# Moving the memory's norm out of the last projections of layer 1 and into its first branch, in a two-block transformer kernel on one core

## The chip, the core and the metric

The kernel runs on one core of a Trainium2 chip. The core has a TensorE for matrix products (PE in the profile, its weight loads PEld), a VectorE (DVE), a ScalarE (ACT), a GpSimd (POOL) and a SyncE (SP), whose queue issues the transfers. The engines run beside each other and wait for each other by semaphores. The metric is the device time of one execution in microseconds, lower is better. The kernel before takes 2549.95 us, the median of three runs that lie between 2549.95 and 2549.96.

## What is computed

The reference is two blocks, one behind the other, over 256 tokens of width 1024, all in float32.

```
x = first_block(x, c, ctx, c_ctx, ...)          # 2 hybrid layers, x and ctx of 256 tokens each
return second_block(x, mem_2, ...)              # 2 layers with a cross attention to a memory
```

A layer of the first block norms its tokens, projects them, and runs three branches: A (a gated recurrent attention with 4 heads), B (a differential attention with 8 heads) and C (a Fourier mix). A branch ends in a merge, a gate times an output projection, and the three merges are summed and go through one last projection `w_out` whose result, gated, is added to x:

```
x = x + gate * merge(y_a, y_b, y_c, mg, w_a_out, w_b_out, w_c_out, w_out)
```

The second block reads a memory of 256 tokens in every layer:

```
def rms_norm(x, g):
    y = xf * lax.rsqrt(jnp.mean(xf * xf, axis=-1, keepdims=True) + EPS)
    return y * g
for i in range(DEPTH):
    h = rms_norm(x, g_mix[i]);  x = x + mixer(h)
    x = x + memory_cross_attention(rms_norm(x, g_xq[i]), rms_norm(mem, g_mem[i]), w_xq[i], w_xkv[i], w_xo[i])
    x = x + swiglu(rms_norm(x, g_ffn[i]), w_gate_up[i], w_down[i])
```

The memory does not depend on x, so its norm can be made at any time once it has arrived. Only the scale `g_mem` differs between the two layers.

## The kernel before

All activations are held transposed: a tensor is eight chunks k of 128 features by the tokens. Every product is made in three passes, with each operand split into a high part (rounded, `wh`, `HYh`) and a low part (the rest, `wl`, `HYl`): high by high, high by low, low by high. A chunk of a projection is so 8 x 3 = 24 matmuls of 256 columns.

The weights are packed into units of up to 1 MB, in the order of use. SP loads a unit into one of two `raw` slots (L2765) when the low part of the unit two before is done. ScalarE rounds it to `wh` (L1332, L1333) when the TensorE has used the unit two before, and VectorE makes `wl` (L1883, L1885). In the programs of both engines this is `used(tag, j)`: the unit has been used, so convert the one two behind it. A unit of a projection is 48 matmuls.

Each engine has its own program, written out in order: `tensor_program`, `scalar_program`, `vector_program`, `pool_program`, `sync_program`. What stands in the order is what runs; nothing is rearranged. An engine waits with `wait_ge` for a named event of another one and with `wait_own` for its own last instruction. The helpers `tt`, `ts`, `stt` (VectorE) and `act` (ScalarE) record nearly every instruction on one line each (L1864, L1868, L1872 and L1322), so the trace is read by tiles. `X` holds x; in layer 1 of the first block its left half is free and holds the memory (`MT`), loaded at the beginning of the layer.

Layer 1 of the first block, as far as it matters here:

- Branch A, heads h = 0 to 3. Per head the TensorE does `a_pick` and `a_s` (scores), two chunks of a gate `a_o` into banks 0 and 1, two chunks `a_z` into the same banks, the products `a_out`, and the next head's `a_qk` and `a_v`. A bank is free for `a_z` when ScalarE has taken its `a_o` with a tanh. Before that tanh ScalarE makes the exponentials of the scores, which wait for VectorE's mask additions (`TM<-PS,colC,T`).
- Its merge, steps j = 0 to 7, one unit each.
- Branch B with its merge, branch C with its merge.
- `project_out`: eight chunks of `w_out`, two to a unit j = 0 to 3. VectorE updates `X` with each chunk (`X<-PS,ada,X`); ScalarE makes from it the high part and the square for the next norm `gmix0`, VectorE the low part and the sum of squares. Chunk k + 2 waits for the update of chunk k.

The memory's norm (`gmem`) also stands in `project_out`: after unit 1 ScalarE squares the memory in four pieces of 512 columns, `memory_root` adds them in three steps and makes the inverse root from the TensorE's `sums`; after chunk 5 the TensorE spreads the root over a bank, and `memory_normed` multiplies the eight chunks (`X<-X,PS`). `memory_high(0)` on ScalarE (eight `HYh<-X,V`) stands ahead of the updates' own high parts of unit 3, and `memory_low(0)` on VectorE (eight `HYl<-X,V,HYh`) at the end of `project_out`. The TensorE then begins the second block with the first key projection of the memory, `memory(0, 0, ...)`, a unit of 48 matmuls that reads these parts chunk by chunk, and the sums of `gmix0` behind it.

## Time and profile before

| | |
|---|---|
| median of 3 runs | 2549.95 us |
| profiled execution, its own time | 2551.46 us |
| its span, first to last instruction | 2549.6 us |
| TensorE busy | 2369.0 us, 93% |
| VectorE busy | 1334.0 us, 52% |
| ScalarE busy | 1027.2 us, 40% |
| GpSimd busy | 252.2 us, 10% |
| mean granted clock of the TensorE | 0.962 |
| share of the TensorE in the chain that ended last | 77% |

A row of the timeline gives the start, the duration, the engine, the line, the operation with what it writes and reads, the count of merged instructions, and in brackets the engine's idle time before it with what ended that. The busy time of the TensorE includes time at a low clock: granted clock 1.00 is 2.4 GHz and 0.50 is 1.2 GHz, and a mean in between is a mix of the two.

### The profile page before, as it was taken

To read this page: it belongs to the slowest core of one execution; us is meant where nothing else is said; L and a number is where in the kernel's file an instruction comes from. 1 tells how busy PE (TensorE), PEld (TensorE's weight loads), DVE (VectorE), ACT (ScalarE), POOL (GpSimd) and SP (SyncE) were. 2 spreads that over 40 slices of the span, in tenths; PEclk is the share of its full clock that TensorE was granted. 3 is DMA by queue.
4 is the path that set the end of the run, shared out by engine and by line. 5 is a ranking of instruction groups with operands and counts; after the bars stand their busy time and mean duration, and the time that the engine had idled before them with its cause. 6 is when DMAs were issued, how large, how long until landed. Compare 5 with 4: busy or idle time off the path is not lost.

```text
span 2549.6 us, 38388 instructions
## 1 busy us (share of the span) xinstructions
PE 2369.0 (93%) x16176; PEld 2128.6 (83%) x16176; DVE 1334.0 (52%) x2731; ACT 1027.2 (40%) x1962; POOL 252.2 (10%) x260
## 2 busy tenths in 40 slices
PE   5999999999979999899999999978888999888998
PEld 3888779888758988699998889978678999767998
DVE  5544424677433223555456654466555555565554
ACT  2433322444422222444434454443444443453543
POOL 1000002222001111000023301201000100100110
PEclk7999999999999999899999999989999999898999
DMA  6321143111224222232332234453132544312544
GB/s 245 101 68 67 57 174 135 67 67 67 83 81 157 75 70 98 74 117 99 129 137 83 70 114 149 166 163 121 51 126 105 182 167 165 114 50 87 179 172 142
DMA packets 50412, 291.45 MB, mean 114 GB/s; under 512 B 8960, under 2 KB 13312, under 8 KB 19072
## 3 DMA queue, kind: packets, MB, share of 16 engines
q1 hardware_dynamic: 50240, 289.00, 31.6%
q8 instruction: 127, 2.08, 0.3%
q14 instruction: 45, 0.37, 0.0%
HBM read 286.89 MB, written 2.36 MB: 113 GB/s over the span
## 4 chain that ended last, share of the span: by engine, by line
PE 77%; DVE 14%; ACT 5%; DMA 2%; issue 1%; POOL 0%; SPq 0%; DVEq 0%; ACTq 0%; POOLq 0%
PE PS L492 75%; DVE wl L1883 2%; PE PS L496 2%; DVE wl L1885 2%; DMA raw<-in_wpk 2%; ACT wh L1332 2%; DVE TM L1864 1%; ACT TM L1322 1%; ACT TMG L1322 1%; DVE colS L1872 1%; DVE HYl L1872 1%; DVE TMG L1872 1%; DVE TM L1872 1%; ACT HYh L1322 1%; DVE colS L2343 1%
## 5 line engine op out<-in xcount | busy, mean ns | idle before, releaser
L492 PE MATMUL PS<-HYh,wh 128*128 128x256 f32 (+1 forms) x3000 | 959.5, 320 | 53.0 <-DVE HYl L1872 35.8
L492 PE MATMUL PS<-HYl,wh 128*128 128x256 f32 (+1 forms) x3000 | 944.3, 315 | 0.0
L492 PE MATMUL PS<-HYh,wl 128*128 128x256 f32 (+1 forms) x3000 | 943.2, 314 | 0.0
L1883 DVE TENSOR_TENSOR wl<-raw,wh 128x1280 fp32r<-128x1280 f32 (+2 forms) x254 | 369.2, 1453 | 596.2 <-ACT wh L1332 596.1
L492 PEld LDWEIGHTS PS<-HYh,wh 128*128 128x128 f32 x3000 | 585.3, 195 | 96.8 <-DVE HYl L1872 38.3
L492 PEld LDWEIGHTS PS<-HYh,wl 128*128 128x128 f32 x3000 | 584.7, 195 | 31.1
L492 PEld LDWEIGHTS PS<-HYl,wh 128*128 128x128 f32 x3000 | 585.6, 195 | 29.5
L1332 ACT ACTIVATE wh<-raw 128x1280 fp32r<-128x1280 f32 (+2 forms) x254 | 306.7, 1208 | 378.3 <-PE PS L492 251.2
L492 PE MATMUL PS<-wh,HYh 128*128 128x256 f32 x1458 | 424.6, 291 | 17.2 <-DVE HYl L1872 11.2
L492 PE MATMUL PS<-wh,HYl 128*128 128x256 f32 x1458 | 415.4, 285 | 0.0
L492 PE MATMUL PS<-wl,HYh 128*128 128x256 f32 x1458 | 415.4, 285 | 0.0
L1322 ACT ACTIVATE TM<-PS 128x512 f32<-128x512 f32 (+4 forms) x339 | 163.7, 498 | 556.7 <-PE PS L492 426.7
L492 PEld LDWEIGHTS PS<-wh,HYh 128*128 128x128 f32 x1458 | 282.2, 194 | 23.0 <-DVE HYl L1872 12.0
L492 PEld LDWEIGHTS PS<-wl,HYh 128*128 128x128 f32 x1458 | 282.4, 194 | 0.3
L492 PEld LDWEIGHTS PS<-wh,HYl 128*128 128x128 f32 x1458 | 282.0, 193 | 0.1
L1885 DVE TENSOR_TENSOR wl<-raw,wh 128x768 fp32r<-128x768 f32 (+2 forms) x254 | 248.1, 977 | 0.0
L492 PE MATMUL PS<-TM 128*128 128x128 f32 (+6 forms) x992 | 218.4, 399 | 19.8 <-ACT rows L1322 8.5
L1333 ACT ACTIVATE wh<-raw 128x768 fp32r<-128x768 f32 (+2 forms) x254 | 206.8, 814 | 0.0
L492 PEld LDWEIGHTS PS<-TM 128*128 128x128 f32 (+2 forms) x992 | 145.5, 194 | 53.9 <-issue 11.9
L2617 POOL TENSOR_TENSOR HYl<-TM,HYh 128x256 fp32r<-128x256 f32 (+2 forms) x56 | 54.9, 982 | 610.9 <-ACT HYh L1322 610.9
L1322 ACT ACTIVATE TMG<-PS 128x512 f32<-128x512 f32 (+2 forms) x121 | 53.4, 441 | 133.2 <-PE PS L492 119.5
L1322 ACT ACTIVATE TMG<-PS,colS 128x512 f32<-128x512 f32 (+1 forms) x104 | 62.1, 603 | 83.2 <-DVE colS L1868 82.9
(181 smaller groups left out, 1793.2 us busy)
## 6 DMA issues: line engine op xcount, KB each, us to landing
raw<-in_wpk SPq DMA_DIRECT2D x235, 1024.0 KB, 4.8
raw<-in_wpk SPq DMA_DIRECT2D x32, 704.0 KB, 4.0
TM<-in_wpk SPq DMA_DIRECT2D x4, 1024.0 KB, 17.4
X<-in_xin SPq DMA_DIRECT2D x1, 2048.0 KB, 9.3
Y<-in_wpk SPq DMA_DIRECT2D x2, 1024.0 KB, 23.1
Y<-bias_d SPq DMA_DIRECT2D x4, 512.0 KB, 9.8
raw<-in_wpk SPq DMA_DIRECT2D x3, 512.0 KB, 3.7
T<-in_tabs SPq DMA_DIRECT2D x1, 1216.0 KB, 15.0
```

Source lines behind the costliest of these rows:

```text
L492: return P.x.matmul(o, l, r, start=start, stop=stop)
L496: return P.x.transpose(o, i, ident[0:p, 0:p])
L1322: return A.x.activation(o, i, f, **kw).then_inc(*act_step.mark(*events))
L1332: A.x.activation(wh[:, s, 0:c], raw[:, r, 0:c], ACT.Copy).then_inc(*hi_split.mark((u, 0)))
L1333: A.x.activation(wh[:, s, c:n], raw[:, r, c:n], ACT.Copy).then_inc(*hi_split.mark((u, 1)))
L1864: return D.x.tensor_tensor(o, a, b, op).then_inc(*dve_step.mark(*events))
L1872: return D.x.scalar_tensor_tensor(out=o, in0=a, scalar=s, in1=b, op0=op0, op1=op1).then_inc(*dve_step.mark(*events))
L1883: D.x.tensor_tensor(wl[:, s, 0:c], raw[:, r, 0:c], wh[:, s, 0:c], ALU.subtract).then_inc(*lo_split.mark())
L1885: D.x.tensor_tensor(wl[:, s, c:n], raw[:, r, c:n], wh[:, s, c:n], ALU.subtract).then_inc(*lo_split.mark(u))
L2343: D.x.reduce_max(mx, src, AX).then_inc(*dve_step.mark())
L2617: return G.x.tensor_tensor(o, a, b, op).then_inc(*pool_step.mark(*events))
```

## The change

The squares of the memory are made in layer 1's branch A, one piece per head, and added up there. They no longer have a place of their own in `TM` (columns 512 to 2560) but use the right halves of `a_g` and `a_z`, which are free in layer 1. Sums, root, spread and normalisation stand in the merge of branch A. In `project_out` the eight high parts come at once, ahead of the first conversion, and one low part with every chunk.

```diff
-        n_sq, n_x = TM[:, 512:2560].rearrange("p (k t) -> p k t", k=8), tm(2560, [8, 256])
+        n_x = tm(2560, [8, 256])
+        g_sum, g_sq = a_g[:, :, 256:512], a_z[:, :, 256:512]
@@ tensor_program, merge
+                    if l == 1 and br == "a" and j == 2:
+                        P.wait_ge(dve_step, ("gmem", "squares", 3))
+                        sums(6, [g_sum[:, 0], g_sum[:, 1]], 256, o1024[:, 0:1], 1, 0, ("gmem", "sums"))
+                    if l == 1 and br == "a" and j == 4:
+                        P.wait_ge(dve_step, ("gmem", "root"))
+                        spread(6, colS[:, 60:62], 256, 1, 0, ("gmem", "spread"))
@@ tensor_program, branch_b
-                free[6] = (dve_step, ("ada", 14)) if l == 0 else (dve_step, ("a_h", l, 3, 3))
+                free[6] = (dve_step, ("ada", 14)) if l == 0 else (dve_step, ("mem", 7))
@@ tensor_program, project_out
-                        if l == 1 and 2 * j + h == 3:
-                            P.wait_ge(dve_step, ("gmem", "squares"))
-                            sums(6, [n_sq[:, 0], n_sq[:, 1]], 256, o1024[:, 0:1], 1, 0, ("gmem", "sums"))
-                        if l == 1 and 2 * j + h == 5:
-                            P.wait_ge(dve_step, ("gmem", "root"))
-                            spread(6, colS[:, 60:62], 256, 1, 0, ("gmem", "spread"))
@@ scalar_program, branch_a, at the end of head h
+                    if l:
+                        A.wait_ge(mem_in, "all")
+                        if h >= 2:
+                            A.wait_ge(dve_step, ("gmem", "squares", h - 1))
+                        act(g_sq if h else g_sum, MT[:, 2 * h:2 * h + 2], ACT.Square, ("gmem", "square", h))
@@ scalar_program, project_out
+                    memory_high(0)
                     for j in range(4):
                         A.wait_ge(projected, ("w_out", l, 2 * j + 1))
                         used("w_out", 4 * l + j)
-                        if j == 1:
-                            for i in range(4):
-                                A.wait_ge(mem_in, "all")
-                                act(n_sq[:, 2 * i:2 * i + 2], MT[:, 2 * i:2 * i + 2], ACT.Square, ("gmem", "square", i))
-                        if j == 3:
-                            memory_high(0)
@@ scalar_program, memory_high
-                    if l:
-                        A.wait_ge(projected, ("w_out", 1, 7))
+                    A.wait_ge(projected, ("w_out", 1, 7) if l else ("m_value", 1, "c", 7))
@@ vector_program, branch_a, at the end of head h
+                        if l and h:
+                            memory_squares(h)
+            def memory_squares(h):
+                D.wait_ge(act_step, ("gmem", "square", 0))
+                D.wait_ge(act_step, ("gmem", "square", h))
+                D.wait_own(dve_step)
+                tt(g_sum, g_sum, g_sq, ALU.add, ("gmem", "squares", h))
@@ vector_program, merge
+                    if l == 1 and br == "a":
+                        if j == 0:
+                            memory_squares(3)
+                        if j == 3:
+                            memory_root()
+                        if j == 5:
+                            memory_normed()
@@ vector_program, project_out
                         if h and (l or j < 3):
                             used("w_out", 4 * l + j)
-                        if l == 1 and k == 3:
-                            memory_root()
-                        if l == 1 and k == 5:
-                            memory_normed()
                         if l == 1:
+                            memory_low(0, k)
...
                 if l == 1:
                     low("gmix0", 7)
-                    memory_low(0)
```

The order of VectorE's instructions around chunks 4 and 5 of `project_out`. `X<-PS,ada,X` is the update of a chunk, the two `wl` rows a conversion, `HYl<-X,V,HYh` a low part, `TM<-TM` an addition of squares. Before:

```order
L1872 SCALAR_TENSOR_TENSOR X<-PS,ada,X 128x256
L1872 SCALAR_TENSOR_TENSOR HYl<-X,V,HYh 128x256
L1864 TENSOR_TENSOR TM<-TM 128x256
L1872 SCALAR_TENSOR_TENSOR X<-PS,ada,X 128x256
L1883 TENSOR_TENSOR wl<-raw,wh 128x1280
L1885 TENSOR_TENSOR wl<-raw,wh 128x768
L1864 TENSOR_TENSOR X<-X,PS 128x256 x8
L1872 SCALAR_TENSOR_TENSOR HYl<-X,V,HYh 128x256
```

And now:

```order
L1872 SCALAR_TENSOR_TENSOR X<-PS,ada,X 128x256
L1872 SCALAR_TENSOR_TENSOR HYl<-X,V,HYh 128x256 x2
L1864 TENSOR_TENSOR TM<-TM 128x256
L1872 SCALAR_TENSOR_TENSOR X<-PS,ada,X 128x256
L1883 TENSOR_TENSOR wl<-raw,wh 128x1280
L1885 TENSOR_TENSOR wl<-raw,wh 128x768
L1872 SCALAR_TENSOR_TENSOR HYl<-X,V,HYh 128x256 x2
L1864 TENSOR_TENSOR TM<-TM 128x256
```

The normalisation of eight is gone, and every chunk has two low parts, the first of the memory and the second of the update before.

The end of `project_out` on VectorE, from the update of chunk 7 on. Before:

```order
L1872 SCALAR_TENSOR_TENSOR X<-PS,ada,X 128x256
L1883 TENSOR_TENSOR wl<-raw,wh 128x1280
L1885 TENSOR_TENSOR wl<-raw,wh 128x768
L1872 SCALAR_TENSOR_TENSOR HYl<-X,V,HYh 128x256
L1864 TENSOR_TENSOR TM<-TM 128x256
L1872 SCALAR_TENSOR_TENSOR HYl<-X,V,HYh 128x256 x9
```

And now:

```order
L1872 SCALAR_TENSOR_TENSOR X<-PS,ada,X 128x256
L1883 TENSOR_TENSOR wl<-raw,wh 128x1280
L1885 TENSOR_TENSOR wl<-raw,wh 128x768
L1872 SCALAR_TENSOR_TENSOR HYl<-X,V,HYh 128x256 x2
L1864 TENSOR_TENSOR TM<-TM 128x256
L1872 SCALAR_TENSOR_TENSOR HYl<-X,V,HYh 128x256
```

Of the memory's eight low parts only that of chunk 7 is left behind the conversion, as the first of the two in its row.

In branch A the additions of squares come between a head's last conversion and the next head's mask additions (`TM<-PS,colC,T`). VectorE, between two heads, now:

```order
L1864 TENSOR_TENSOR HYl<-TM,HYh 128x2x256
L1883 TENSOR_TENSOR wl<-raw,wh 128x1280
L1885 TENSOR_TENSOR wl<-raw,wh 128x768
L1864 TENSOR_TENSOR TM<-TM 128x2x256
L1872 SCALAR_TENSOR_TENSOR TM<-PS,colC,T 128x128 x4
```

The fourth row is new; before, the mask additions followed the conversion.

## Rows read from the trace of the kernel before

**Rows 1.** By stretch: length, busy PE PEld DVE ACT POOL, PEclk, DMA share, GB/s

```profile
1641.00:1656.00 15.00, 15.00 (x127) 15.00 (x127) 8.87 (x15) 7.40 (x13) 2.32 (x3) 1.00 0.50 178
1656.80:1660.80 4.00, 1.47 (x13) 1.27 (x12) 3.27 (x5) 0.93 (x3) 1.58 (x1) 1.00 0.10 41
1669.20:1691.60 22.40, 16.05 (x108) 15.85 (x108) 14.44 (x34) 8.91 (x16) 0.00 (x0) 0.77 0.29 102
1691.60:1706.60 15.00, 7.22 (x48) 7.25 (x49) 9.56 (x20) 6.61 (x14) 0.00 (x0) 0.77 0.99 256
1245.00:1249.00 4.00, 3.91 (x20) 3.91 (x21) 1.60 (x3) 0.94 (x3) 0.00 (x0) 0.57 0.00 0
```

**Rows 2.** Timeline of the TensorE: start, duration, what, count, idle before, releaser

```profile
1675.52 1.87 PE L492 MATMUL PS<-T,TM 128*128 128x1 f32 x8 [6.33 <-DVE TM L1864]
...
1699.38 0.55 PE L492 MATMUL PS<-HYh,wh 128*128 128x256 f32 x1 [7.81 <-DVE HYl L1872]
...
1699.95 0.42 PE L492 MATMUL PS<-HYh,wl 128*128 128x256 f32 x1
1700.16 0.41 PE L492 MATMUL PS<-HYh,wh 128*128 128x256 f32 x1
...
1706.61 0.95 PE L492 MATMUL PS<-T,TM 128*128 128x1 f32 x8
...
1245.09 1.07 PE L496 MATMUL PS<-T,TM 128*128 128x128 f32 x4 [2.85 <-ACT TM L1322]
```

**Rows 3.** Timeline of VectorE in the last projections of layer 1

```profile
1664.78 1.49 DVE L1883 TENSOR_TENSOR wl<-raw,wh 128x1280 fp32r<-128x1280 f32 x1 [0.82 <-ACT wh L1332]
1666.19 0.95 DVE L1885 TENSOR_TENSOR wl<-raw,wh 128x768 fp32r<-128x768 f32 x1
1667.06 0.48 DVE L1872 SCALAR_TENSOR_TENSOR HYl<-X,V,HYh 128x256 fp32r<-128x256 f32 x1
1667.45 0.48 DVE L1872 SCALAR_TENSOR_TENSOR X<-PS,ada,X 128x256 f32<-128x256 f32 x1
1668.04 0.48 DVE L1872 SCALAR_TENSOR_TENSOR HYl<-X,V,HYh 128x256 fp32r<-128x256 f32 x1
1668.62 0.42 DVE L1864 TENSOR_TENSOR TM<-TM 128x256 f32<-128x256 f32 x1
...
1673.19 2.27 DVE L1864 TENSOR_TENSOR TM<-TM 128x512 f32<-128x512 f32 x3
...
1689.00 2.73 DVE L1864 TENSOR_TENSOR X<-X,PS 128x256 f32<-128x256 f32 x8
...
1698.35 3.65 DVE L1872 SCALAR_TENSOR_TENSOR HYl<-X,V,HYh 128x256 fp32r<-128x256 f32 x9
```

**Rows 4.** Timeline of ScalarE in the last projections of layer 1

```profile
1658.41 0.42 ACT L1322 ACTIVATE HYh<-Y 128x256 fp32r<-128x256 f32 x1 [1.10 <-POOL Y L2617]
1663.47 1.27 ACT L1332 ACTIVATE wh<-raw 128x1280 fp32r<-128x1280 f32 x1 [4.64 <-PE PS L492]
...
1669.61 1.27 ACT L1332 ACTIVATE wh<-raw 128x1280 fp32r<-128x1280 f32 x1 [2.72 <-DMA raw<-in_wpk]
...
1671.52 2.17 ACT L1322 ACTIVATE TM<-X 128x512 f32<-128x512 f32 x4
```

**Rows 5.** Timelines of VectorE and ScalarE in branch A and its merge

```profile
1182.05 0.95 DVE L1885 TENSOR_TENSOR wl<-raw,wh 128x768 fp32r<-128x768 f32 x1
1182.91 1.12 DVE L1872 SCALAR_TENSOR_TENSOR TM<-PS,colC,T 128x128 f32<-128x128 f32 x4
...
1269.04 1.49 DVE L1883 TENSOR_TENSOR wl<-raw,wh 128x1280 fp32r<-128x1280 f32 x1 [3.07 <-ACT wh L1332]
...
1186.35 0.42 ACT L1322 ACTIVATE TM<-PS 128x256 f32<-128x256 f32 x1
1187.15 0.39 ACT L1322 ACTIVATE TM<-PS 128x256 f32<-128x256 f32 x1 [0.38 <-PE PS L492]
```

**Rows 6.** Issue to landing of the unit issued at 1697.0, by the raw tile

```profile
DMA to landing us min/median/max: 9.2/9.2/9.2
```

More of the change, by code:

```diff
@@ L2294, in memory_root @@
             def memory_root():
-                D.wait_ge(act_step, ("gmem", "square", 0))
-                for i in range(1, 4):
-                    D.wait_ge(act_step, ("gmem", "square", i))
-                    D.wait_own(dve_step)
-                    tt(n_sq[:, 0:2], n_sq[:, 0:2], n_sq[:, 2 * i:2 * i + 2], ALU.add, ("gmem", "squares"))
                 D.wait_ge(pe_step, ("gmem", "sums"))
@@ L2306, in memory_normed, with memory_low @@
                     tt(MT[:, k], MT[:, k], bank(6)[:, 0:256], ALU.mult, ("mem", k))
-            def memory_low(l):
-                for k in range(8):
+            def memory_low(l, *ks):
+                for k in ks:
                     D.wait_ge(act_step, ("mem_hi", l, k))
@@ L2447, in self_attention @@
                     if i == 0:
-                        memory_low(1)
+                        memory_low(1, *range(8))
                 D.wait_ge(pe_step, ("ab_q_spread", 1))
```

## The prediction

> **What bounds the kernel now.** I read three views in this order: the busy time by stretch, the timeline of the TensorE around the last projections of layer 1, and then the timelines of the two engines that feed it. The kernel is bound by the TensorE: away from waits it issues a matmul of 256 columns every 0.12 us (127 in 15 us, clock 1.00) [rows 1], and every other engine has idle time. So a change is worth what it takes out of the TensorE's own idle time and low clock. The stretch from 1669.2 to 1706.6 us holds the two places that the diff touches. The reader is to see two things in [rows 1, 2]. The first: after chunk 3 of the output projection the TensorE stands still for 6.33 us, then does the sums of the memory's squares, and ends chunk 7 at 1691.6. The second: it stands still again for 7.81 us until the first low part of the memory is there, and ends the first key projection (48 matmuls) at 1706.6. Both stretches have a mean clock of 0.77, between the two levels of 1.2 and 2.4 GHz [rows 1]. The work in between is 4 chunks and one unit of 48, that is 6 x 24 matmuls x 0.12 = 17.3 us; 37.4 us pass. At most 20.1 us can be had here.
>
> Why it waits is in [rows 3, 4]. The squares are made on ScalarE at 1671.5, after a conversion that had waited until 1669.6 for its transfer; VectorE adds them in three steps (2.27 us). The second wait is for ScalarE's eight high parts and VectorE's eight low parts (one row of 9, 3.65 us), both queued behind a conversion.
>
> **The change part by part.**
>
> *Taken out of the projections.* No squares, sums, root or normalisation is left between chunk 3 and chunk 6. Chunk 4 can start at 1669.2, if its weights and its bank are there: the weights were converted from 1664.8 to 1667.1 [rows 3], and VectorE's update of chunk 2 (1667.45 in the row) was out by 1668. So 6.33 us of idle, the sums at a cold clock, and the slow matmuls behind them go.
>
> *High parts at once.* Eight ScalarE instructions stand ahead of the first conversion now. ScalarE's last merged high part starts at 1658.4, and the conversion waits until 1663.5 for the TensorE (4.64 us of idle) [rows 4]. Eight at about 0.41 take 3.3 us, so they end at 1662.1. Cost nothing; the cover has 1.4 us left.
>
> *Low parts by chunk.* This is what is late next, so I put VectorE's queue together from start to start. From [rows 3]: update to low part 0.59, low part to addition 0.58, low part to update 0.39, first half of a conversion to the second 1.41, second half to the next 0.87. A low part of the memory without a wait takes 0.40 (3.65 / 9), and the next instruction, which waits for its own engine, comes 0.58 behind it. An update or an addition starts its successor 0.09 before its own end where that doesn't wait (0.48 against 0.39), so addition to update is 0.33 to 0.35. An even chunk is 0.40 + 0.58 + 0.58 + 0.35 = 1.91 us, an odd one with its conversion 0.39 + 1.41 + 0.87 + 0.58 + 0.58 + 0.35 = 4.18, together 6.1, against 5.76 of the TensorE for two chunks. VectorE falls behind a little. Run through from 1660.6 with ScalarE's conversions as they stand, the updates start at 1668.0 (chunk 2), 1669.9, 1674.7, 1676.6, 1680.8, 1682.7 (chunk 7). Chunk 6 needs the update of chunk 4, out at 1675.2 where the TensorE arrives at 1675.0: it ends chunk 7 at 1681.0. The key projection needs the update of chunk 6: it starts at 1681.35. Its matmuls take the memory in order of k; the last low part stands behind the conversion that follows chunk 7 (1683.1 and 1684.5, then 1685.4) and is out at 1685.9, where the TensorE wants it at 1683.9: a wait of 2.0 us. Then 27 matmuls: the unit ends at 1689.15. Before it ended at 1706.6. **Gain 17.5 us.** The bound from one side is 20.1 (no new wait), from the other 10.9 - 0.5 = 10.4 (the second wait stays whole: 22.4 us less 4 x 2.88, less the small waits).
>
> *Squares in the first branch.* Four ScalarE instructions of 128x512 at about 0.6 (2.17 / 4) [rows 4]; each stands where ScalarE then waits over 1.4 us, so they cost nothing. Three additions of VectorE at 0.7 to 0.8 (2.27 / 3). The third falls in the merge. The first two stand between the second half of a conversion and the mask additions of the next head (1182.1 and 1182.9 [rows 5]), and what follows moves by 0.8: ScalarE's exponentials, then its tanh of gate chunk 0 at 1186.35, which frees bank 0 only at 1187.6 where it was 1186.8. The TensorE wants that bank when the other chunk ends, at about 1187.0 (its tanh starts at 1187.15). So it waits some 0.7 us where it waited for nothing, in two heads: **1.4 us lost.** The bounds are 0, if the bank is asked for later than I read, and 2 x 0.83 = 1.7. Behind ScalarE wait only the next tanh and a conversion. A conversion takes 3.7 us from the end of a unit to the weights (1663.5 to 1667.1 [rows 3, 4]) and its unit is wanted 5.76 after it: 2 us of slack.
>
> *Sums, root, normalisation in the merge.* The sums are 8 passes in 0.95 us at the full clock (those of the next norm at 1706.6 [rows 2]); with the half as many passes of the spread, 0.45, that is **1.3 us lost** there, with 0.9 and 2.3 (the same sums took 1.87 at the low clock) as bounds. They are already counted as gone from the projections. VectorE idles 3.07 us in every unit of the merge [rows 5]; the root (12 small ones, 0.2 each, 2.35 us) and the normalisation (8 in 2.73 us [rows 3]) each stand alone in such a gap. The cover is 0.3 us at the tighter one, and a conversion late by less than 2 us still meets its unit. Nothing. The wait for bank 6 in front of the second branch is moved to the last normalised chunk, which is out two units earlier.
>
> *Transfers.* Everything on SP's queue that hangs on a conversion comes with it. The one that can be late is the unit that stands behind the four bias blocks: before it took 9.2 us [rows 6]. Now it goes out at 1685.5, when its conversion is done, and closer behind those blocks: I add 2 us, an estimate, and it is in by 1696.7, where ScalarE wants it at about 1696.1 (1689.15, the norm's sums 0.95, a unit 5.76, a copy). The slack of 2 us takes that up. Nothing.
>
> **Sum.** 17.5 - 1.4 - 1.3 = 14.8 us. The profiled execution has a span of 2549.6 and took 2551.46, 1.5 above the median of the runs; the difference is taken off the median: 2549.95 - 14.8 = **2535.1 us**.
>
> The clock, as a test of the 2.0 us wait: after 2.5 us of idle at 1657 the stretch 1656.8 to 1660.8 (1.47 us busy) still has 1.00 [rows 1]; after the 2.85 us at 1245 [rows 2] the next 4 us have 0.57. My waits are shorter than the first, so I keep the full clock; two gaps of that size (1245, 1657) now come at another time and may fall either way, about 2 us each.
>
> **Rivals.**
> *The clock falls in the new wait.* The key projection lost 7.23 - 5.76 = 1.5 us to it before [rows 2]; 27 matmuls all at half speed would be 2.5. 2537. For it speaks that three short waits fall within 8 us.
> *The second wait stays.* VectorE's low parts and ScalarE's copies collide more than I have them, and the TensorE still waits as long at the key projection: gain 10.4, less 2.7: 2542.2. Against it: seven of eight low parts now have a slot ahead of chunk 7's end.
> *No new waits.* The last low part is in time and the heads hide the additions: 2.0 + 0.5 + 1.4 more: 2531.2.
> *The transfer hides it.* Chunk 4 waits for weights instead, and the moved work is pure cost: 2549.95 + 2.7 = 2552.6. Against it: 1667.1 in the row.
> *Slower, by the clock.* VectorE needs 6.1 us for two chunks where the TensorE needs 5.76, so from chunk 4 on the TensorE has a short wait in every chunk. If that pattern held the clock at its low level until the fourth projection of the second block is done (12 chunks, 288 matmuls at 0.213, the distance of the two rows at 1700 [rows 2], for 0.12), it would cost 26.8 us: 2561.9. It decides from the point where it lasts beyond 6 chunks or so. Against it stand the short waits of 0.3 us beside a wait of 2.5 us at clock 1.00 in the row.
> The Trainium skill (TensorE: Matmul & The Clock Gate, A second HAM failure mode: psum-queue depth-cycling) describes a kernel in which frequent short idles between groups of matmuls made the clock go to and fro; by that rule this rival would be the likely one. The trace here shows the full clock across a longer wait than any that I expect, so I give it little.
>
> **How the numbers follow.** My forecast 0.68 (its own range 2532.5 to 2537.5), the clock in the new wait 0.12, the second wait 0.08, no new waits 0.06, the transfer 0.03, slower by the clock 0.03. The range to hold 8 in 10 takes in the two coins of the clock and leaves out the last two and a part of the second wait: 2530.5 to 2541. Within 0.2% (5.1 us, about what can be told from no change) lies only the transfer case: 0.03; slower 0.03; faster 0.94.
>
> **What would show it.** After: no TensorE wait between chunk 3 and chunk 5 of layer 1's projections; all eight chunks end within 23.5 us of the start of the first; one wait of about 2 us inside the first key projection, ended by a low part on VectorE; 17 to 18 us less up to its end; two waits of 0.7 us in the last two heads of the branch, ended by ScalarE's tanh; 1.3 us of sums and spread in the merge. I am wrong if the TensorE still waits over 4 us at the key projection, if the stretch from 1669 on shows a clock under 0.9, or if the branch and its merge grow by over 4 us.

## The result, and where the time went

The changed kernel took 2535.56 us (median of 4 runs, 2533.26 to 2538.65) beside a median of 2549.95 for the kernel before (a fourth run of that one took 2555.34). The ratio is 0.994, with a 95% interval of 0.9924 to 0.9955. Five more runs of it, made later beside the experiments, gave a median of 2535.24 (2534.43 to 2539.52), and the ratio there is 0.9934 (0.9921 to 0.9946): the kernel before had a median of 2552.6 in that round, 17.4 more. The forecast was 2535.1.

The profiled execution of the changed kernel is the slowest of the first four: it took 2538.65, its span is 2536.8 against 2549.6, 12.8 less. Before the spans are read, one has to know how much of a difference belongs to the edit. I laid the TensorE instructions of the two traces against each other, one by one, and read how much later or earlier the same instruction starts after the change (positive is later):

| stretch, in the times of before | changed kernel | the same kernel, profiled again |
|---|---|---|
| start to 1095 us (nothing changed in it) | +1.6 | +0.2 |
| 1095 to 1285, branch A's last heads and the merge's start | +2.4 | +0.9 |
| 1285 to 1640 | 0.0 | -1.1 |
| 1640 to 1727, the projections and the first key projection | -17.8 | -17.4 |
| 1727 to the end | +0.9 | +0.4 |
| sum, from unrounded terms | -12.8 | -17.0 |

The second column is the run "again" of the next section. Only the fourth line is the edit's gain and the second its price. In the first column the price is read at a like clock (both kernels had 3.4 us of low clock in the second stretch); in the second column that low clock is absent, which takes 1.5 us off the price. I put the rest down to the clock, granted otherwise from run to run. For the third line that is argued only: of the twelve profiles in which the norm is early, nine have 13.7 us of low clock there and start 0.9 to 1.3 us less late behind it, and three have 17.1 us like the kernel before and the one other profile with the norm in its old place. Whether the edit has a part in that, no run here tells.

By stretch the profile after shows this (columns as in [rows 1]):

```profile
1640.00:1673.20 33.20, 30.67 (x256) 30.47 (x255) 20.23 (x31) 18.02 (x33) 5.03 (x5) 1.00 0.56 199
1673.20:1692.90 19.70, 17.83 (x146) 17.31 (x145) 16.63 (x29) 10.26 (x18) 0.00 (x0) 1.00 0.72 220
```

The second line, with the PEclk third from its end, runs from the end of chunk 3 to the end of the key projection, and it answers to the third and fourth of [rows 1]: 19.7 us where 37.4 passed. The granted clock is 1.00, the higher of the two levels, where it was 0.77. The TensorE's timeline there (start, duration, what, count, idle before, releaser), answering to [rows 2]:

```profile
1663.61 0.39 PE L493 MATMUL PS<-HYh,wh 128*128 128x256 f32 x1 [2.53 <-DVE HYl L1864]
...
1689.55 0.38 PE L493 MATMUL PS<-HYh,wh 128*128 128x256 f32 x1 [1.79 <-DVE HYl L1872]
...
1692.87 0.95 PE L493 MATMUL PS<-T,TM 128*128 128x1 f32 x8
```

These are the start of chunk 0, the one wait left behind it, and the next norm's sums. The waits of 6.33 and 7.81 us are gone. What released the wait of 1.79 us stands in VectorE's timeline, which answers to [rows 3]:

```profile
1684.84 1.06 DVE L1872 SCALAR_TENSOR_TENSOR HYl<-X,V,HYh 128x256 fp32r<-128x256 f32 x2
1686.01 0.42 DVE L1864 TENSOR_TENSOR TM<-TM 128x256 f32<-128x256 f32 x1
1686.35 0.47 DVE L1872 SCALAR_TENSOR_TENSOR X<-PS,ada,X 128x256 f32<-128x256 f32 x1
1686.75 1.48 DVE L1883 TENSOR_TENSOR wl<-raw,wh 128x1280 fp32r<-128x1280 f32 x1
1688.14 0.95 DVE L1885 TENSOR_TENSOR wl<-raw,wh 128x768 fp32r<-128x768 f32 x1
1689.01 1.07 DVE L1872 SCALAR_TENSOR_TENSOR HYl<-X,V,HYh 128x256 fp32r<-128x256 f32 x2
```

The row at 1686.35 is the update of chunk 7, the next two are the last conversion, and the last row holds the memory's last low part and one of the query norm's. The low part could have started at 1686.75 and started at 1689.01.

ScalarE's timeline, answering to [rows 4]:

```profile
1662.75 3.29 ACT L1323 ACTIVATE HYh<-X,V 128x256 fp32r<-128x256 f32 x8
1667.51 1.27 ACT L1333 ACTIVATE wh<-raw 128x1280 fp32r<-128x1280 f32 x1 [1.46 <-PE PS L493]
...
1701.58 1.27 ACT L1333 ACTIVATE wh<-raw 128x1280 fp32r<-128x1280 f32 x1 [1.27 <-DMA raw<-in_wpk]
```

The high parts take 3.29 us and 1.46 us of idle are left behind them. The last row is the unit whose transfer stands behind the bias blocks. By SP's timeline it is issued at 1689.12, and it takes longer than the 9.2 us of [rows 6]:

```profile
1683.50 2.76 SPq L2816 DMA_DIRECT2D Y<-bias_d  x4
1689.12 8.46 SPq L2771 DMA_DIRECT2D raw<-in_wpk  x2
```

```profile
DMA to landing us min/median/max: 12.4/12.4/12.4
```

The price is in the branch and the merge. The TensorE waits 0.32 us for the tanh in heads 2 and 3, where it did not wait before, and it does the sums in the merge:

```profile
1188.42 0.28 PE L493 MATMUL PS<-HYh,wl 128*128 128x256 f32 x1
1189.01 0.39 PE L493 MATMUL PS<-HYh,wh 128*128 128x256 f32 x1 [0.32 <-ACT TM L1323]
1189.24 0.28 PE L493 MATMUL PS<-HYl,wh 128*128 128x256 f32 x1
...
1264.20 0.95 PE L493 MATMUL PS<-T,TM 128*128 128x1 f32 x8
```

The bracket counts idle from the end of the matmul before, and so says less than a wait costs. From start to start the first two steps here are 0.59 and 0.23 us, where neighbours have 0.12: each of the two waits costs 0.58.

### The profile page after: what moved, and what is told of

Same layout as the page of the kernel before. It is cut to its first block, busy times and chain, and to the rows that moved or that the text cites. A ratio compares the mean times of both kernels' runs of the same rounds, so it can differ in the third digit from the quotient of the medians.

```text
span 2536.8 us, 38388 instructions
## 1 busy us (share of the span) xinstructions
PE 2371.2 (93%) x16176; PEld 2128.4 (84%) x16176; DVE 1333.5 (53%) x2731; ACT 1027.0 (40%) x1962; POOL 252.4 (10%) x260
## 4 chain that ended last, share of the span: by engine, by line
PE 77%; DVE 14%; ACT 5%; DMA 2%; issue 1%; POOL 0%; SPq 0%; DVEq 0%; ACTq 0%; POOLq 0%
PE PS L493 75%; DVE wl L1883 3%; DVE wl L1885 2%; PE PS L497 2%; ACT wh L1333 2%; ACT TM L1323 1%; DMA raw<-in_wpk 1%; DVE TM L1864 1%; ACT TMG L1323 1%; DVE colS L1872 1%; DVE HYl L1872 1%; DVE TM L1872 1%; DVE TMG L1872 1%; DVE colS L2349 0%; ACT HYh L1323 0%
## 5 line engine op out<-in xcount | busy, mean ns | idle before, releaser
L493 PE MATMUL PS<-wh,HYh 128*128 128x256 f32 x1458 | 425.4, 292 | 17.2 <-DVE HYl L1872 11.2
## 6 DMA issues: line engine op xcount, KB each, us to landing
TM<-in_wpk SPq DMA_DIRECT2D x4, 1024.0 KB, 17.5
Y<-in_wpk SPq DMA_DIRECT2D x2, 1024.0 KB, 23.4
T<-in_tabs SPq DMA_DIRECT2D x1, 1216.0 KB, 15.2
```

Source lines behind the costliest of these rows:

```text
L493: return P.x.matmul(o, l, r, start=start, stop=stop)
```

## The experiments

"Up to 1727" below is always the stretch from 1640 to 1727 us in the times of before, laid against it instruction by instruction as in the table. The changed kernel has 17.8 us less there, and 17.4 in its second profile. Where differences of a microsecond are asked for, these stretches decide. The medians do not, since the runs of one kernel spread over some 5 us (thirteen of the kernel before, in one round, over 11.8).

**The same kernel again.** No edit.

> The changed kernel once more, unaltered, beside the experiments. Theory: the profile of the changed kernel was already 1.72 us later than before's at 1095 us, ahead of every changed instruction, because the clock fell in other places there; that is a matter of the run and not of the edit. So its runs spread over some 5 us again (2533 to 2539), the median lies between 2534 and 2538, and in the new profile the lateness at 1095 us is another number than 1.72, while the stretch from 1640 to the sums of the next norm is again 17.8 shorter (within 0.3), with a wait of about 1.8 us for the last low part. Rival: the edit itself moves the clock in the first half; then the lateness at 1095 us is 1.7 again.

Measured: 2535.24 (2534.43 to 2539.52). The lateness at 1095 us is +0.2 and not +1.6 (the 1.72 of the expectation is what it was some 7 us ahead of that point), so the edit is not its cause. Up to 1727 it has 17.4 less. The new thing lies at the idle 2.85 us ahead of the merge's last turned head [rows 2]. First the changed kernel, by stretch, then the same kernel again:

```profile
1242.00:1246.00 4.00, 2.98 (x25) 2.78 (x23) 2.39 (x13) 1.21 (x5) 0.00 (x0) 1.00 0.52 219
1246.00:1250.00 4.00, 2.17 (x16) 2.17 (x17) 1.69 (x8) 2.32 (x5) 0.00 (x0) 0.90 0.00 0
1250.00:1254.00 4.00, 4.00 (x26) 4.00 (x25) 1.26 (x2) 1.11 (x2) 0.00 (x0) 0.67 0.00 0
```

```profile
1242.00:1246.00 4.00, 1.56 (x14) 1.36 (x12) 2.44 (x13) 1.06 (x4) 0.00 (x0) 1.00 0.16 66
1246.00:1250.00 4.00, 3.59 (x30) 3.59 (x31) 2.26 (x4) 1.80 (x5) 0.00 (x0) 1.00 0.00 0
1250.00:1254.00 4.00, 4.00 (x36) 4.00 (x35) 2.36 (x2) 2.64 (x4) 0.00 (x0) 1.00 0.02 4
```

One program, and the clock falls once (0.90 and 0.67) and once not (1.00). It costs 1.5 us (+0.84 against -0.64 between 1235 and 1262 us). The second profile has one wait more that I had forecast: 0.27 us at chunk 6, for VectorE's update of chunk 4. It comes from a transfer. The unit issued at 1660.97 (in the times of before) landed after 8.6 us here and after 7.4 in the first profile, so ScalarE's conversion, and behind it VectorE's queue, was 0.4 us later.

```profile
1675.23 0.38 PE L493 MATMUL PS<-HYh,wh 128*128 128x256 f32 x1 [0.27 <-DVE X L1872]
```

**Only the norm early.** The high parts stand behind the last conversion and the low parts at the end, as before.

```
 ScalarE, project_out
-    memory_high(0)
     for j in range(4): ... used("w_out", 4 * l + j)
+        if j == 3: memory_high(0)
 VectorE, project_out
-                            memory_low(0, k)
 ...
                     low("gmix0", 7)
+                    memory_low(0, *range(8))
```

> The changed kernel with its norm in the branch and the merge, but with the high parts behind the last conversion and all low parts at the end, as in the kernel before. Theory (two waits in a row, each with its own cause): the wait after chunk 3 goes, the one at the key projection stays near 7.8 us. The 22.4 us for chunks 4 to 7 become 11.5: 10.9 less; the additions, sums and spread cost 2.4: 8.5 us less than before, 2541.5. Rival (one chain: VectorE ends it, and taking away the first wait only lengthens the second): the second wait grows by what the first loses, and the kernel is 2.4 us slower than before.

Measured: 2540.52 (2539.58 to 2543.71), ratio 0.9952 (0.9933 to 0.997). The TensorE's timeline:

```profile
1689.33 0.55 PE L493 MATMUL PS<-HYh,wh 128*128 128x256 f32 x1 [7.81 <-DVE HYl L1873]
```

The second wait stands at 7.81, to the hundredth what it was, so the two waits are separate and the rival with one chain is refuted. Up to 1727 it has 8.4 less, not 10.9. The rest is clock: 3.4 us of low clock behind the wait of 2.52 ahead of chunk 0, and 5.3 us of it under the key projection where before had 3.2. The first, by stretch:

```profile
1659.00:1663.00 4.00, 4.00 (x25) 4.00 (x26) 0.67 (x2) 0.00 (x0) 0.00 (x0) 0.69 0.49 165
```

**Only the parts early.** The kernel before, with its norm in the projections. `memory_high` waits for `("m_value", 1, "c", 7)`, as in the changed kernel.

```
 ScalarE, project_out
+                        if j == 3: memory_high(0)
                         A.wait_ge(projected, ("w_out", l, 2 * j + 1)); used(...)
 ...
-                        if j == 3: memory_high(0)
 VectorE, project_out
+                        if l == 1 and k == 7: memory_low(0)
                         if h and (l or j < 3): used("w_out", 4 * l + j)
 ...
-                    memory_low(0)
```

> The kernel before, its norm within the projections as it was, but the eight high parts ahead of ScalarE's last conversion and the eight low parts directly behind VectorE's last update. Theory: the wait after chunk 3 stays 6.3 us. The normalisation ends at 1691.7, the high parts run from 1689.4 to 1692.7 beside it, the low parts start at 1692.3, and the key projection starts near 1692.7 where it was at 1700: 7.3 us less than before, 2542.7; the last low part (1695.6) is in time. Rival: the conversions, now behind 3.3 us of parts on both engines, come too late for the second key projection, and the wait moves there: 3 us less at most. Together with the run that has only the early norm it says whether the two gains add up (8.5 + 7.3 + the 1.8 us that the last low part costs against 17.8 - 2.4 measured).

Measured: 2548.32 (2545.89 to 2552.84), ratio 0.9985 (0.9975 to 0.9995); 4.2 less up to 1727, not 7.3. The TensorE's and then VectorE's timeline:

```profile
1679.65 1.87 PE L492 MATMUL PS<-T,TM 128*128 128x1 f32 x8 [5.95 <-DVE TM L1863]
...
1699.59 0.36 PE L492 MATMUL PS<-HYh,wh 128*128 128x256 f32 x1 [3.72 <-DVE HYl L1871]
```

```profile
1693.29 2.73 DVE L1863 TENSOR_TENSOR X<-X,PS 128x256 f32<-128x256 f32 x8
...
1698.57 0.48 DVE L1871 SCALAR_TENSOR_TENSOR X<-PS,ada,X 128x256 f32<-128x256 f32 x1
1698.96 3.25 DVE L1871 SCALAR_TENSOR_TENSOR HYl<-X,V,HYh 128x256 fp32r<-128x256 f32 x8
```

The normalisation (2.73 us) holds up VectorE's updates, so the one of chunk 7 starts at 1698.57 and the low parts behind it. The wait shrinks to 3.72 and not to nothing. I had counted the low parts from the end of chunk 7, as if VectorE were free then. Together the halves give 8.4 + 4.2 = 12.6 and the whole 17.4 to 17.8: the low parts can only be spread over the chunks if the norm is done ahead of them. Of the waits of 6.33 and 7.81 the halves take away 6.3 and 4.5, together 10.8, and the whole 12.1 to 12.4; that is 1.3 to 1.6 of the 5 us between the sum of the halves and the whole. The larger part goes with the clock: each half alone keeps 13.7 us of low clock between 1640 and 1707 us (17.1 before), and the whole keeps none.

**Each low part twice.**

```
                         if l == 1:
                             memory_low(0, k)
+                            D.wait_own(dve_step)
+                            memory_low(0, k)
```

> The changed kernel with each of the memory's eight low parts made twice in layer 1's projections (the second waits for the first and writes the same numbers), which adds about 0.6 us of VectorE a chunk: 7.3 us for two chunks where TensorE needs 5.76. Theory (short waits don't lower the clock in this stretch): TensorE waits up to 0.75 us in each of the chunks from 4 on, the granted clock stays 1.00 from 1669 to the end of the key projection, and the stretch is 3 to 4.5 us longer than in the changed kernel, VectorE's lag and no more: 2538.5 to 2540. Rival (by the pattern of short waits): the clock falls to its low level for the stretch and beyond, and it is 10 us or more longer.

Measured: 2538.54 (2537.19 to 2539.67), ratio 0.9943 (0.9923 to 0.9964). Up to 1727 it has 12.9 less, that is 4.5 to 4.8 longer than the changed kernel. The TensorE's timeline and the stretches:

```profile
1675.83 0.39 PE L493 MATMUL PS<-HYh,wh 128*128 128x256 f32 x1 [1.12 <-DVE X L1872]
...
1682.95 0.39 PE L493 MATMUL PS<-HYh,wh 128*128 128x256 f32 x1 [1.10 <-DVE X L1872]
...
1688.57 0.58 PE L493 MATMUL PS<-HYh,wh 128*128 128x256 f32 x1 [2.84 <-DVE HYl L1872]
```

```profile
1668.80:1685.70 16.90, 14.68 (x118) 14.10 (x117) 15.68 (x30) 10.00 (x17) 0.00 (x0) 1.00 0.53 191
1685.70:1689.70 4.00, 1.16 (x6) 1.14 (x6) 3.68 (x6) 0.48 (x2) 0.00 (x0) 0.82 1.12 217
1689.70:1693.70 4.00, 4.00 (x29) 4.00 (x28) 0.48 (x1) 0.23 (x1) 0.00 (x0) 0.75 1.13 222
```

The waits add up to 5.06 us, 3.0 more than in the second profile of the changed kernel (0.27 + 1.80); the 3.4 us of low clock behind the wait of 2.84 account for most of the rest. The theory had waits of up to 0.75 us, a full clock to the end of the key projection and 3 to 4.5 us; it was short on all three. Across the two waits of 1.1 us the clock stayed at 1.00. The rival in which short waits hold it low did not come with waits of this size and number. The rule that stood beside it in the prediction, of frequent short idles (the Trainium skill, TensorE: Matmul & The Clock Gate, A second HAM failure mode: psum-queue depth-cycling), was not seen at work in this run.

**The last low part first.**

```
+                        if l == 1 and k == 7: memory_low(0, 7)
                         if h and (l or j < 3): used("w_out", 4 * l + j)
                         if l == 1:
-                            memory_low(0, k)
+                            if k < 7: memory_low(0, k)
```

> The changed kernel, with the memory's last low part (k = 7) ahead of VectorE's last conversion of the projections. Theory (the wait of 1.79 us inside the first key projection is the queue place of this one instruction, behind 2.3 us of conversion): the low part starts at 1686.8 where it was 1689.0, TensorE wants it at 1687.8, the wait goes, the conversion is 0.5 us later and still in time: 1.8 us less than the changed kernel in the stretch from 1640 to the sums of the norm (15.9 us from chunk 4's start to the end would be 18.1 where 19.9 are now). Rival: another instruction is as late (the low part of the query's norm, or the conversion, or its weights for the second key projection), and the wait shows up again within 6 us: no gain. Second rival: the clock takes it back.

Measured: 2534.46 (2533.13 to 2534.96), ratio 0.9927 (0.9914 to 0.9941). Up to the norm's sums it has 2.0 to 2.4 less than the changed kernel's two profiles. Behind them 1.6 come back. The TensorE's timeline, then ScalarE's:

```profile
1701.44 0.36 PE L493 MATMUL PS<-wh,HYh 128*128 128x256 f32 x1 [1.37 <-DVE wl L1885]
```

```profile
1697.63 1.27 ACT L1333 ACTIVATE wh<-raw 128x1280 fp32r<-128x1280 f32 x1 [3.22 <-DMA raw<-in_wpk]
```

The first rival held. The wait is gone, and the TensorE comes earlier to the unit whose transfer stands behind the bias blocks. Net it is 0.4 to 0.8 up to 1727.

**The two additions moved** behind the root of the next head.

```
                     root(..., ("a_root", l, h), eps=64 * EPS)
+                    if l and h >= 2: memory_squares(h - 1)
 ...
-                        if l and h: memory_squares(h)
```

> The changed kernel, with the two VectorE additions of squares that stood between two heads of branch A put behind the root of the next head, where VectorE idles 5.4 us. Theory (each costs TensorE 0.57 us because the mask additions, the exponentials and the tanh that frees its bank come later by 0.6): both waits of 0.32 us at 1189 and 1230 us are gone, the two heads are 1.14 us shorter, nothing else changes: 1.1 us less than the changed kernel. Rival: the ScalarE squares ahead of the exponentials (0.6 us each) are what makes the head late, and the additions are hidden: no change.

Measured: 2533.97 (2532.99 to 2539.01), ratio 0.9929 (0.9916 to 0.9941). Between 1180 and 1235 us it stands at 0.00 against before, where the changed kernel has +1.15: the additions alone are the cause, and the squares of ScalarE cost nothing. But its profile has the low clock behind the idle of 2.85 us, +0.81 where the kernel again has -0.64, and so the gain is not to be seen in the sum at 1285 us (+1.2 against +0.9). All seven profiles without the delay in both heads, that of before among them, show that fall of the clock; of the seven with it, six do not. So the two additions cost 1.15 us, and in six profiles of seven the clock gave 1.5 back. I can't say why; that the later arrival decides it is only argued.

**The idle time filled**, the sums ahead of the last turned head.

```
 TensorE, merge, j == 0
                         gate(u, 0, 0)
+                        P.wait_ge(dve_step, ("gmem", "squares", 3)); sums(6, [g_sum[:, 0], g_sum[:, 1]], ...)
                         last(3)
 (and no sums at j == 2)
 ScalarE: squares 0 and 1 behind head 0, 2 behind head 1, 3 behind head 2
 VectorE: additions 1 and 2 behind the roots of heads 1 and 2, 3 between the products of head 3
```

> The changed kernel with the squares one head earlier, their additions in gaps of VectorE, and the sums in TensorE's idle 2.85 us ahead of the merge's last turned head; the last low part stays where it is. Theory: 1.1 + 0.9 = 2.0 us less than the changed kernel, all of it between 1140 and 1280 us, and up to 1 us more from the clock behind the shortened idle; the wait of 1.8 us in the key projection is untouched. Rival: the idle passes the third addition on, 1.3 less.

> The changed kernel with three edits: the last low part ahead of the last conversion; the squares one head earlier and their three additions in gaps of VectorE of 2.4 to 5.4 us; the sums on TensorE in the middle of its idle 2.85 us ahead of the merge's last turned head, where they were 0.87 us on its path. Theory: 1.8 + 1.1 + 0.9 = 3.8 us less than the changed kernel, and up to 1 us more if the shorter idle keeps the clock up where it had a mean of 0.57 over the next 4 us. About 2531 against 2535. Rival: the idle of 2.85 us isn't shortened by the sums, but the clock falls there all the same, or falls elsewhere: between 2.5 and 3.8 less. Rival that it is not faster: the third addition, put between two products of the last head, delays the head's end by 0.7 us, which the wait of 2.85 us passes on whole: 3.1 less.

Measured: 2534.12 (2533.54 to 2535.64) for the first, ratio 0.9925 (0.9908 to 0.9943), and 2535.06 (2533.21 to 2536.45), 0.993 (0.9918 to 0.9943), for the second, which has the last low part first too. The TensorE's timeline of the first:

```profile
1242.15 0.95 PE L493 MATMUL PS<-T,TM 128*128 128x1 f32 x8
...
1245.16 1.12 PE L497 MATMUL PS<-T,TM 128*128 128x128 f32 x4 [2.06 <-ACT TM L1323]
```

The sums lie in the idle time, which shrinks from 2.85 to 2.06. Against the kernel with only the additions moved that is 1.0 us less (-0.17 against +0.81), as forecast. The clock still falls there. In the second kernel 1.6 us come back at the next weights, as with the last low part alone. No gain of either can be told by the medians.

The first kernel shows one thing more. It has the wait of 1.80 us in the key projection like the changed kernel, but here the clock falls behind it, by the TensorE's timeline and by stretch:

```profile
1684.98 0.48 PE L493 MATMUL PS<-HYh,wh 128*128 128x256 f32 x1 [1.80 <-DVE HYl L1873]
```

```profile
1685.00:1689.00 4.00, 4.00 (x21) 4.00 (x22) 1.40 (x3) 0.00 (x0) 0.00 (x0) 0.57 1.13 222
```

Up to 1727 it has 16.3 less where the changed kernel has 17.4 and 17.8, so that fall costs 1.1 to 1.5 us.

**The bias blocks a unit later.**

```
-                if u == place["ab_k", 0]:
+                if u == place["ab_k", 0] + 1:
```

> The changed kernel, with the four bias blocks one unit later and nothing else. Theory (the transfer behind the bias blocks, 1.27 us late for ScalarE, is absorbed by the slack of its unit because TensorE itself is 1.8 us late by the wait for the last low part): ScalarE's wait for the transfer goes and TensorE's times do not move: 0. Rival: the late transfer cost TensorE time that I did not see: 0.5 to 1.3 us less.

> The changed kernel with the last low part first and the four bias blocks one unit later. Theory: both waits (1.8 us for the low part, 1.6 us for the weights that took its place) are gone, and up to 1727 the stretch is 19.6 us shorter than before, against 18.2 with the low part alone and 17.4 to 17.8 in the changed kernel. Rival as for the first run: 18.2 again.

> The kernel with the squares a head earlier, the sums in the idle time and the last low part first, and now the four bias blocks on SP's queue one unit later, behind the transfer of the weights that follow them. Theory (behind the last low part the next limit is that transfer: it took 11.9 us to land behind the bias blocks, where its neighbours take 5, so its conversion began 3.2 us late and TensorE waited 1.4 us for the weights): the transfer lands 5 to 6 us after its issue, the wait of 1.4 us goes, and the stretch from 1640 to 1727 is 19.4 to 19.8 us shorter than before where it was 18.2. 1.6 less than without the edit, unless the clock takes it. Rival: the unit behind the bias blocks is late now, and the wait shows up one unit later: no gain.

Measured: alone 2535.1 (2532.46 to 2536.47), ratio 0.9939 (0.9925 to 0.9952), and 17.2 less up to 1727: nothing, as the theory says. The next unit's weights are 0.40 us late there, and the wait for the root behind them is 3.30 instead of 3.82. With the last low part first 2530.87 (2526.82 to 2532.55), 0.9919 (0.9905 to 0.9932). With the idle filled as well 2532.31 (2530.23 to 2535.66), 0.9927 (0.9915 to 0.994). In both pairs the wait shows up one unit later, as the rival has it, and up to 1727 they have 15.9 and 15.2 less, short of the theory's 19.6 and of the rival's 18.2. The TensorE's and ScalarE's timelines of the kernel with the last low part first:

```profile
1708.07 0.36 PE L493 MATMUL PS<-HYh,wh 128*128 128x256 f32 x1 [2.15 <-DVE wl L1885]
```

```profile
1702.93 1.27 ACT L1333 ACTIVATE wh<-raw 128x1280 fp32r<-128x1280 f32 x1 [3.42 <-DMA raw<-in_wpk]
```

The next unit is the late one. But now the wait falls ahead of the one that the TensorE has for the root of the next norm. VectorE has that root behind one more conversion. In the kernel again it idled 2.52 us in front of that conversion, and here it goes straight on to it:

```profile
1710.14 1.49 DVE L1883 TENSOR_TENSOR wl<-raw,wh 128x1280 fp32r<-128x1280 f32 x1 [2.52 <-ACT wh L1333]
```

```profile
1707.85 1.48 DVE L1883 TENSOR_TENSOR wl<-raw,wh 128x1280 fp32r<-128x1280 f32 x1
```

The first row is of the kernel again, the second of this one. Of the wait of 3.82 us that the kernel again has for the root at 1715.20, 0.23 are left. From 1727 to 1800 us this kernel then has 7.5 less than the kernel again (-7.4 against +0.1); 3.6 are that wait, and the rest goes with 8.4 us of low clock there instead of 20.5. Up to 1800 us, both stretches together, it has 23.4 less, and 20.8 with the idle filled; without the blocks moved the same two kernels have 17.7 and 17.3. A late transfer costs less when it overlaps a wait that is there anyway. The ratios don't carry that far: 0.9927 and 0.9919 for the pair with the last low part first, 0.993 and 0.9927 for the other, with intervals that overlap.

**The version the runs point to**: last low part first, bias blocks a unit later, additions moved.

> The changed kernel with the last low part first, the bias blocks one unit later and the two additions behind the roots: the version that the runs so far point to. Theory: the terms add up: 1.14 us less than the same without the additions moved (2530.9), so 2529.7, if the clock doesn't take it; against the changed kernel (2535.2) 5.5 us less, of which about 3.9 from waits taken away up to 1727 us and from the wait for the norm's root behind it, and the rest from the clock between 1727 and 1800 us. Rival: the gain behind 1727 us was the clock's own luck in one run; then 2532 to 2534.

Measured: 2531.7 (2529.24 to 2533.68), ratio 0.9919 (0.9906 to 0.9933). The rival's 2532 is nearer than the theory's 2529.7. The two heads are 1.15 us shorter again, but the low clock at 1245 us is there again too and takes 1.4 back. It is the same as without the additions moved, some 3.5 us below the changed kernel (2535.24), though the intervals of the two ratios (0.9919 and 0.9934) overlap, and faster than the kernel before by 0.8%. The TensorE's timeline shows that the wait for the root is not gone in this run, only shorter, behind the same wait of 2.15:

```profile
1715.11 0.66 PE L493 MATMUL PS<-T,colS 128*64 128x128 f32 x8 [1.72 <-DVE colS L1864]
```

Here the clock stays up behind the wait of 2.15, and the root's wait is shorter by 2.1: that is the overlap without the clock's part. In the two runs ahead of this one the clock fell there, the TensorE was slower, and it came to the root with 0.2 and 0.3 us to wait. This profile has up to 1727 only 14.8 less, because a transfer came late that had not been on my list, that of the unit issued at 1660.97. It landed after 9.9 us. ScalarE's conversion waited for it, and then chunk 6 for the update of chunk 4:

```profile
1670.39 1.27 ACT L1333 ACTIVATE wh<-raw 128x1280 fp32r<-128x1280 f32 x1 [4.05 <-DMA raw<-in_wpk]
```

```profile
1676.01 0.38 PE L493 MATMUL PS<-HYh,wh 128*128 128x256 f32 x1 [1.62 <-DVE X L1872]
```

## Why the prediction was right, point by point

- **What bounds the kernel.** Right. The TensorE's idle time and low clock were the gain, and nothing else moved.
- **Gain 17.5.** Measured 17.8 and 17.4. The run with only the norm early leaves the second wait at 7.81, as the lower bound took it, but it gains 8.4 and not 10.4: that bound left out the clock. The whole gain needs both halves.
- **VectorE's queue from start to start.** It held to a few tenths: the wait in the key projection stands at the place and for the low part named, 1.79 in the bracket, and taking it away brought 2.0 to 2.4 (forecast 2.0). The wait of 0.25 at chunk 6 is 0.27 in the second profile and absent in the first; the 0.35 at the key projection's start was in neither. The step took ScalarE's conversions "as they stand", and that is its weak place: the conversion ahead of chunk 6 hangs on the unit issued at 1660.97. With a landing after 7.4, 8.6 and 9.9 us in three profiles, chunk 6 waited 0, 0.27 and 1.62 us.
- **High parts hidden.** 3.29 us with 1.46 left (forecast 3.3 and 1.4).
- **Additions, 1.4.** Measured 1.15, and the run with them moved has 0.00: right in cause, a little high in size. Each head loses 0.58 where I had 0.7; the bracket shows 0.32 of it.
- **Sums and spread, 1.3.** 1.3: the whole price to 1285 is 2.4 and the additions are 1.15 of it. The root and the normalisation cost nothing: from 1285 to 1640 the changed kernel loses 0.0, with the same 17.1 us of low clock as before.
- **The transfer behind the bias blocks.** I had 11.2 us and 0.6 late. The first profile has 12.4 and 1.27, the second 11.4 and 0.24, so 0.6 lies within what one program does and 11.2 just below it. The effect of none is confirmed by the run with the blocks moved. It was absorbed by the wait for the last low part, though, as well as by the unit's own slack. With that wait gone the transfer costs the TensorE 1.4 us.
- **The clock.** It stayed at 1.00 behind the new wait in both profiles of the changed kernel. Five profiles have this wait of 1.8 us, and in one of them, that with the idle filled, the clock fell behind it, at a cost of 1.1 to 1.5 us; it also fell when I made the wait 2.84. So the rival "the clock falls in the new wait" is not refuted. It came once in five, and my 0.12 for it was not far off; that the forecast kept it out was in part luck. The two places that I called coins (1245 and 1657 us) were such: the clock at the first fell in one profile of the changed kernel and not in the other, and at the second it fell behind the wait of 2.5 us in one profile of fourteen, that with only the norm early.
- **The span.** My sum gave 14.8 less. Against before's profile the changed kernel's two profiles have 12.8 and 17.0 less; between 1095 and 1285 and up to 1727 together they have 15.4 and 16.5. In the second, 1.5 us of the difference are the low clock that did not come at 1245 us, and 1.1 lie between 1285 and 1640. The forecast had the first as a coin and no term for the second, and six of the twelve profiles with the norm early show both, so they may not be scatter alone.
- **The median.** That it came within 0.5 us is partly luck. The forecast hangs on a median of 2549.95 from three runs; the kernel before had medians of 2550.96 to 2552.6 in the four later rounds. Measured in one round, the difference is 17.4 us and not 14.8, which is nearer to the second profile than to my sum.

Of the other rivals, the second wait staying and the one that is slower by the clock were tested by making them, and are not what the change does. That the transfer hides the gain is refuted by the changed kernel's own profile: chunk 4 waits for nothing. The rival without new waits was made too, in part: taking the wait for the low part away brought 0.4 to 0.8 us up to 1727 and not 2.0, because the next weights were late.

## What to carry to other kernels

When two waits stand in a row on the busiest engine, ask whether one chain causes both. Here they were separate, and yet the halves of the change gave 12.6 us and the whole over 17: only the whole let the work spread over gaps, and only with the whole was there no low clock in the stretch. Add up the queue of the helping engine from start to start; that gave the place and size of the next wait to 0.2 us. Ask also what transfer stands behind that queue: one landing of 9.9 us instead of 7.4 put 1.6 us of wait on the busiest engine. And before you chase a wait of 2 us, look one and two units behind it: here a transfer stood there with the same lateness, and what counted was into which other wait it fell.

## What the hardware did that I had not expected

- A program that is the same up to 1095 us was 1.6 us later there in one profile and 0.2 in another; by the clock records the first had 75 us of low clock up to there and the second 65. The amount of low clock alone doesn't give the lateness: the profiles with only the norm early and with each low part twice had 37.5 us of it up to there and were only 0.3 and 0.1 us earlier than before. The nine runs of the changed kernel reach from 2533.26 to 2539.52, so an edit worth 1 to 2 us is told only by its stretch.
- The same idle time of 2.85 us was followed by a clock of 0.67 in one profile and 1.00 in another of one program, at a cost of 1.5 us.
- A unit queued behind four blocks of 512 KB landed after 12.4 us in the changed kernel, after 11.4 in its second profile and after 12.9 with the additions moved, where the page has a median of 4.8 for transfers of its size. With the blocks a unit later, the next unit took 12.5.
- Two waits of 1.1 us within 8 us left the clock at 1.00, and one of 2.84 us behind them did not. But the size of a wait doesn't settle it: one of 1.8 us left the clock up in four profiles and not in a fifth, and one of 2.15 us left it up in one profile and not in two.
